# Projections: token classes ordered by the completing sum, and the high part stored from the part's place

## The reference

```python
def dilated_mixer(x, w_qkv, w_o, t5_table):
    qkv = (x @ w_qkv).reshape(B, S, N_DIL, 3, N_HEADS_A, HEAD_DIM)   # N_DIL = 3
    for g, (win, dil) in enumerate(DILATIONS):                        # dil = 1, 4, 16
        o, l = _dilated_branch(qkv[:, :, g, 0] * HEAD_DIM ** -0.5, qkv[:, :, g, 1], qkv[:, :, g, 2], ...)

def neighbourhood_mixer(x, w_qkv, w_o, rpb):
    qkv = (x @ w_qkv).reshape(B, rows, GRID_W, 3, H, Dh)
```

## Time and profile before

| | us |
|---|---|
| three runs: median (lowest, highest) | 5923.65 (5918.23, 5925.77) |
| the profiled execution | 5922.98 |
| its span, first to last instruction | 5921.1 |
| stage qa (window 20 to 1537) | 1517 |
| stage qb (window 3516 to 4054) | 538 |
| PE busy, whole span | 5487.6 (93%) |
| DVE busy, whole span | 3837.4 (65%) |
| ACT busy, whole span | 2870.3 (48%) |

### The profile page before, as it was taken

The page is one execution under the profiler, slowest core; times in us unless marked ns, Lnnn a source line. Parts: engine busy times, 40 slices in busy tenths (PEclk is TensorE's granted clock), DMA queues, the critical chain, the costliest instruction groups (busy, mean ns, idle before and its releaser), DMA issues. The chain is left out here.

```text
span 5921.1 us, 101032 instructions
## 1 busy us (share of the span) xinstructions
PE 5487.6 (93%) x31546; PEld 4721.1 (80%) x31547; DVE 3837.4 (65%) x6597; ACT 2870.3 (48%) x4819; POOL 1273.0 (21%) x957
## 2 busy tenths in 40 slices
PE   7999999999899979699999879998999897999997
PEld 5888788898899978578787737988999685788773
DVE  5678877778555558676766457874444555655795
ACT  3343443445477766265555314444666213645661
POOL 2010020000000000064655331200000003544583
PEclk9999999999999989899999989999999897999998
DMA  6776766667799976387887475653443426876987
GB/s 184 207 209 194 199 215 200 195 176 198 239 318 311 312 245 180 133 287 269 327 293 288 171 291 178 201 155 126 157 122 115 132 82 212 302 255 239 342 305 280
DMA packets 888282, 1309.42 MB, mean 221 GB/s; under 512 B 186014, under 2 KB 547149, under 8 KB 887948
## 3 DMA queue, kind: packets, MB, share of 16 engines
q1 hardware_dynamic: 596316, 839.10, 43.8%
q0 software_dynamic: 77168, 294.67, 14.6%
q10 hardware_dynamic: 214464, 171.31, 9.8%
HBM read 974.87 MB, written 348.87 MB: 224 GB/s over the span
## 5 line engine op out<-in xcount | busy, mean ns | idle before, releaser
L508 PE MATMUL qa_ps_out<-qa_x_hi,qa_w_hi 128*128 128x512 f32 x1344 | 533.2, 397 | 38.7 <-DVE qa_w_lo L644 22.3
L508 PE MATMUL qa_ps_out<-qa_x_hi,qa_w_lo 128*128 128x512 f32 x1344 | 528.9, 394 | 0.0
L508 PE MATMUL qa_ps_out<-qa_x_lo,qa_w_hi 128*128 128x512 f32 x1344 | 528.8, 393 | 0.0
L545 ACT ACTIVATE qa_w_hi<-qa_w_whole 128x1024 fp32r<-128x1024 f32 x180 | 191.4, 1063 | 423.0 <-DVE qa_w_whole L635 276.2
L508 PE MATMUL qa_ps_out<-qa_w_hi,qa_x_hi 128*128 128x256 f32 x1344 | 383.4, 285 | 8.4 <-DVE qa_w_lo L644 8.2
L508 PE MATMUL qa_ps_out<-qa_w_hi,qa_x_lo 128*128 128x256 f32 x1344 | 381.5, 284 | 0.0
L508 PE MATMUL qa_ps_out<-qa_w_lo,qa_x_hi 128*128 128x256 f32 x1344 | 381.4, 284 | 0.0
L1984 POOL TENSOR_TENSOR b_ex_w_lo<-b_ex_w_raw,b_ex_w_hi 128x1024 fp32r<-128x1024 f32 x128 | 348.4, 2756 | 132.7 <-ACT b_ex_w_hi L1981 130.5
L1984 POOL TENSOR_TENSOR a_ex_w_lo<-a_ex_w_raw,a_ex_w_hi 128x1024 fp32r<-128x1024 f32 x128 | 345.5, 2731 | 139.0 <-ACT a_ex_w_hi L1981 137.0
L2478 DVE CUSTOM_DVE_ANT_0 ga_minus_s<-ga_ps_s,ga_bias 128x512 f32<-128x512 f32 (+1 forms) x256 | 193.9, 758 | 266.5 <-PE ga_ps_s L2421 254.5
L1003 PE MATMUL da_ps_o<-da_v_two,da_probT 128*128 128x130 f32 x2560 | 356.0, 278 | 1.1 <-DMA da_v_two<-v 1.1
(11 more groups left out here) (442 smaller groups left out, 15774.4 us busy)
## 6 DMA issues: line engine op xcount, KB each, us to landing
a_ex_w_raw<-w SPq DMA_DIRECT2D x128, 1024.0 KB, 12.6
b_ex_w_raw<-w SPq DMA_DIRECT2D x128, 1024.0 KB, 12.6
qa_w_raw<-w_qkv_a SPq DMA_DIRECT2D x144, 512.0 KB, 5.1
a_ex_w_raw<-w POOLq DMA_DIRECT2D x66, 1024.0 KB, 9.2
b_ex_w_raw<-w POOLq DMA_DIRECT2D x66, 1024.0 KB, 8.8
da_q_cross<-qT SPq DMA_DIRECT2D x48, 1024.0 KB, 8.8
da_k_parts<-kT SPq DMA_DIRECT2D x48, 1024.0 KB, 10.0
ys<-qa_x_rows POOLq DMA_DIRECT2D x64, 512.0 KB, 4.3
```

Source lines behind the costliest of these rows:

```text
L508: done = pe.matmul(out, stationary, moving, start=(k == 0 and i == 0), stop=(k == KH - 1 and i == 2))
L545: act.activation(w_hi[:, p % W_RING], src, ACT.Copy).then_inc(w_hi_done, 1)
```

## The change

The completing add (L654) now writes every completed result into `stage`, for q and k too, and makes the class order itself: it reads `part` and the PSUM bank with a step of r numbers and writes in sequence. ACT then makes the high part from `stage` back into the result's place in `part`, without a stride, and issues the stores from `part`. DVE makes the low part from `stage` and `part`, also without a stride. With that:

- ahead of L594 ACT no longer waits for `stored[u]` nor for `low_done`;
- DVE waits ahead of the completing add for the high and low part of the unit two before (or for its stores, if that was of kind 2);
- `begin` of a block's first product waits in addition until all stores of the block before have landed, since they read `part`. This holds behind blocks of every kind.

```diff
@@ begin
                         act.wait_ge(low_done, low_units(n))
+                        for i in range(2):
+                            act.wait_ge(stored[i], 32 * 4 * n)
@@ finish
-                        if e >= 2:
-                            act.wait_ge(stored[u], 32 * (e // 2))
-                        if low >= 2:
-                            act.wait_ge(low_done, low - 1)
-                        act.activation(in_class_order(r, stage[:, u, :].bitcast(F32R), True),
-                                       in_class_order(r, result(seq, side, u), False), ACT.Copy, scale=scale_of(kind)
-                                       ).then_inc(high_done, 1)
+                        act.activation(result(seq, side, u).bitcast(F32R), stage[:, u, :], ACT.Copy,
+                                       scale=scale_of(kind)).then_inc(high_done, 1)
...
-                            act.dma_start(dst, stage[HD * i:HD * i + HD, u, :].rearrange("c (r i) -> c r i", r=r)
+                            act.dma_start(dst, result(seq, side, u)[HD * i:HD * i + HD].rearrange("c (r i) -> c r i", r=r)
@@ gather_parts
-                    if kind == 2:
-                        e = unit(n, m, u)
-                        if e >= 2:
+                    e = unit(n, m, u)
+                    if e >= 2:
+                        before = (e - 2) // 8
+                        if blocks[before][2] == 2:
                             dve.wait_ge(stored[u], 32 * (e // 2))
-                            dve.wait_ge(low_done, low_units(n))
-                        out = stage[:, u, :]
-                    else:
-                        out = result(row, col, u)
-                    add(out, result(row, col, u), bank, ALU.add)
+                        else:
+                            dve.wait_ge(high_done, low_units(before) + (e - 2) % 8 + 1)
+                            dve.wait_ge(low_done, low_units(before) + (e - 2) % 8 + 1)
+                    r = classes[g] if kind < 2 else 1
+                    add(in_class_order(r, stage[:, u, :], True), in_class_order(r, result(row, col, u), False),
+                        in_class_order(r, bank, False), ALU.add)
@@ low_parts
-                            out=in_class_order(r, stage_lo[:, u, :].bitcast(F32R), True),
-                            in0=in_class_order(r, result(row, col, u), False), scalar=scale_of(kind),
-                            in1=in_class_order(r, stage[:, u, :], True), op0=ALU.mult, op1=ALU.subtract
+                            out=stage_lo[:, u, :].bitcast(F32R), in0=stage[:, u, :], scalar=scale_of(kind),
+                            in1=result(row, col, u), op0=ALU.mult, op1=ALU.subtract
```

More of the change, by code:

```diff
@@ L697, in low_parts @@
                     row, col = COMPLETES[m]
-                    r = classes[g]
                     for u in range(2):
```

## The result

| | before | after |
|---|---|---|
| median of five runs each, on the same chip, us | 5918.89 | 5940.63 |
| lowest, highest, us | 5913.63, 5925.77 | 5936.35, 5949.42 |
| ratio to before, 95% interval | | 1.0033 [1.0020, 1.0046] |
| profiled execution, us (its span) | 5922.98 (5921.1) | 5936.35 (5934.5) |

The change makes the kernel slower by 0.33%, about 20 us. Forecast were +29 us and 5952.

The account below looks back on a forecast made before the run. PE, busy 93% of 5921.1 us, was taken as the bound, with ACT and DVE a second chain beside it. 18 + 8 + 6 - 3 = +29 us on 5922.98 gave 5952 us, range 5908 to 5985.

Parts of the forecast that it names:

- the added wait: Before each block's first begin, ACT waits for the last block's stores to land; paid at 35 + 11 block starts.
- the removed waits: ACT's 63.7 us of waits for its own stores go; DVE's waits for the high part allowed 3 us more gain.
- The blocks with r = 4 or 8: Sixteen block starts in qa, +1.3 us each or +21; about 3 fall in slack, leaving +18 us.
- the ping-pong's gain: In products 3 and 6, shorter high parts end ACT's chain 1.0 us sooner and DVE's 0.87; nothing in 4 and 5.
- rival 1: No difference within 12 us: landings near 2.6 us, first pass free, 0 to +6 from the passes; 5926, chance 0.19.
- The point of decision: Store landing time of 2.56 us, at which the chain of a block with r = 4 or 8 doesn't change.
- The starts of the second passes: Once in qa, once in qb: x_hi queues behind the begin waiting for stores of v; +3 us each, +6.
- The early blocks: First blocks of the first pass, r = 1, landings up to 10.5 us: between nothing and 17 us, taken as +8.
- The zero in quiet r = 1 blocks: In qb and qa's second pass the begin goes to at most 11 us behind, hidden by the limit: zero.
- the 12.0: Limit in us that a block's begin may lie behind the block's start, given when PE needs w_lo.
- rivals 3 and 4: Much slower: the add takes 1.5 us, 5992, chance 0.07; high part doesn't get to 629 ns, 5982, chance 0.03.
- Rival 2: Faster: the removed waits made the chain late, half or more of 38 us of stalls go; 5903, chance 0.16.

Follow-up runs that it names:

- e1: The kernel before with only the added wait: each block's first begin also waits until all stores of the last block have landed; 6012.77 us, ratio 1.0131 to before.
- e8: The changed kernel with ACT's two removed waits (stores and low part) put back ahead of each high part; 5957.3 us, ratio 1.0052 to before.
- e2: The changed kernel with the new wait left out behind blocks of v; 5936.8 us, ratio 1.0006 to before.
- e4: The changed kernel with first copies reordered around w_hi and stores counted per result, so each copy waits only for its own; 5890.35 us, ratio 0.9929 to before.
- e5: The kernel before with POOL's eight bias-tile loads moved from the first blocks to the second pass; 5934.73 us, ratio 1.0005 to before.

## Why the prediction came out right, and where it didn't

Direction, size and range held: +29 forecast, +20 measured, and what costs and what pays were named rightly. That the size came out is in part luck: each of the three parts of the sum was too small, the cost as well as the gains, and the errors nearly cancelled:

| | forecast, us | measured, us |
|---|---|---|
| the added wait, unpaid (16 x (3.9 + 0.65 - 1.34) - 3 + 8 + 6) | +62 | +78 (e1) |
| the new accesses (16 x 1.87) | -30 | -47 (e1 to e8) |
| the removed waits | -3 | -11 (e8 to after), not clear of noise |
| sum | +29 | +20 |

(The forecast's terms are regrouped; the last measured one is what is left to the result.)

**The blocks with r = 4 or 8** (+18 forecast, -5.0 and +0.2 in two traces). The step that failed is the size of two terms: the ping-pong's gain, and l, the time from issue to landing of a block's last store. Means over the twelve blocks of q or k with r = 4 or 8 that follow another such block of the same branch, in us after the block's first begin, worked out from the trace's records of the high parts (L594 before, L590 after), the begins and the stores:

| | last high part ends | next begin | l, last store |
|---|---|---|---|
| before | 39.51 | 41.04 | 3.90 |
| e1 | 39.56 | 44.08 | 3.84 |
| e8 | 37.10 | 41.27 | 3.45 |
| after | 36.57 | 40.54 | 3.26 |

The prediction let the last high part end 1.87 us sooner and left l at 3.9, so the begin came out 1.3 later. It ends 2.94 us sooner, and l is 3.26: 36.57 + 0.65 + 3.26 = 40.5, 0.5 us sooner than before. The formula for the begin was right, two numbers in it weren't. Of the 2.94, 2.4 are there in e8, with the old waits. The ends of DVE's low parts show in which products: in e8 product 3 gains 1.04 (0.87 forecast), and product 5, where "nothing is won", 0.4 more. The fall of l was rival 1's argument, high and low stores no longer issued together; the runs show it, not why. The point of decision, 2.56 for l, became 3.6 with the true gain, and l is below it. DVE's wait for the high part fell by 42 us. The prediction had called nearly all of its 49.4 us priced; priced were 16 x (0.79 + 1.17), some 31.

**The starts of the second passes** (+6 forecast, +20.2 and +17.2). The failed step is the place: begins of the v block ahead of the pass wait too, and x_hi queues behind them there already. e2 gives all of it back.

**The early blocks** (+8 forecast, +14.1 and +14.2). The second trace of before is itself 10.2 us above the first, so between 4 and 14 us are the change's. The fourth block alone shows it best: 38.9 and 39.9 us before, 47.9 and 48.1 after, 48.3 in e1 and 48.9 in e2, which have the wait too; but 42.1 in e8, which has it as well. The bounds, 0 and 17, held.

**The zero in quiet r = 1 blocks** held: the six such blocks behind the start of qa's second pass sum to the same length, as do those of qb; the begin lies at most 11.6 us behind the block's start in the six and 8.6 in qb's, inside the 12.0. **Add, high and low part** came out to 0.01 us; rivals 3 and 4 fall. **Rival 2** (faster by the removed waits) falls: they are worth some 11 us of the 63.7. **Rival 1** was right that l falls, if to 3.26 and not to 2.6, and would have had the r = 4/8 blocks; it failed on "the first pass costs nothing" and on 0 to +6 at the passes. **The clock**: in the stalled early blocks the granted clock is 0.90 and 0.93 of full speed (0.96 and 1.00 before), a part of their length that the sum had only in its range.

**The range**: its upper end adds up to 5922.98 + 29 + 9 + 11 + 10 = 5982, and not to 5985; the result is far from either.

Of the signs that were named, ACT's waits moved to the begin and DVE's wait for w_hi rose, as said. PE's wait for w_lo was to rise by about 25 us, in the first pass and with r = 8; it rose by 9.5. Put down to the blocks, it went from 6.1 to 17.8 us in the early ones and fell from 16.8 to 15.4 in the r = 8 ones. That was the sign that the r = 4/8 term was too large, if a weak one: in the second trace of before the early blocks have 13.3.

Open stays how the 20 us are made up to the last. In the trace of after qa and qb together are 27.3 us longer, from first to last matmul, and the stages between and behind them, which the change doesn't touch, 9 and 5.5 us shorter. Two traces of one kernel differ there by 1 to 3 us only; over all twelve traces the same code between qa and qb took 1987 to 2004 us. No run shows why.

## What to carry to other kernels

Before a wait is put ahead of an instruction, list what is queued behind that instruction and who needs it soonest; here the same wait cost 78 us ahead of w_hi, and with w_hi ahead of it the whole change is 42 us faster than the kernel before. Let a wait count what the buffer's reader really is: no wait behind v, whose stores read another buffer, won 16 us by itself (e2). Counting per result was measured only together with the new order (e4). A transfer that makes others land late won nothing when it was moved; look first for a stretch in which nothing waits for a landing.

## What the runs showed of the hardware

- A step in PSUM added nothing on DVE here: the add with an SBUF and a PSUM operand at a step of 16 bytes takes 1071 ns, the old low part with one SBUF operand at that step 1073. The Trainium skill (Advanced Engine Details and Errata, section Memory Cachelines) has finer lines in PSUM than in SBUF and speaks of matmuls; for an add on DVE this trace shows no sign of them. At 32 bytes the add takes 1138.
- ACT pays for a step of 16 bytes in its source as DVE does: 1127 ns against 629 without one.
- The last stores of a block landed sooner in the new order (l from 3.90 to 3.45 in e8 and 3.26 in after). That high and low stores of a unit no longer go out together is a reason that was argued, not tested.
- Loads of the bias tiles that land 7.9 to 15.3 us after their issue lengthen the landings of small stores beside them: up to 10.5 us for ACT's stores of 140 to 250 us, 4.9 with the loads elsewhere (e5), and PE's stall in the third block of qa (3.21 us) is gone.
